# Stick-breaking attention: the running sums from rounded halves of the softplus instead of fp32 matmuls over a running total

## The reference

```
z = einsum('bqhd,bkhd->bhqk', q[:, q0:q1], k[:, :q1]) * scale
strict = k_pos[None, :] < q_pos[:, None]
log_1m = where(strict, -softplus(z), 0.0)
later = cumsum(log_1m, axis=3, reverse=True) - log_1m
w = where(strict, exp(log_sigmoid(z) + later), 0.0)
out = einsum('bhqk,bkhd->bqhd', w, v)
```

## Time and profile before

| | |
|---|---|
| time, median of 3 runs | 2959.64 us (2959.38 to 2963.29) |
| span of the profiled execution | 2957.5 us |
| the profiled execution's own time | the page gives its span alone |
| TensorE busy | 2864.2 us, 97% of the span |
| DVE, ACT, POOL busy | 36%, 43%, 39% of the span |
| DMA | 84 GB/s over the span |
| stick-breaking stage, layer 1 | from about 262 to 330 us of the span |
| stick-breaking stage, layer 2 | from about 1117 to 1184 us |

### The profile page before, as it was taken

The page is one execution under the profiler, slowest core; times in us unless marked ns, Lnnn a source line. Parts: engine busy times, 40 slices in busy tenths (PEclk is TensorE's granted clock), DMA queues, the critical chain, the costliest instruction groups (busy, mean ns, idle before and its releaser), DMA issues.

```text
span 2957.5 us, 39307 instructions
## 1 busy us (share of the span) xinstructions
PE 2864.2 (97%) x14662; PEld 2299.9 (78%) x14662; DVE 1067.7 (36%) x1405; ACT 1257.9 (43%) x1825; POOL 1141.6 (39%) x288
## 2 busy tenths in 40 slices
PE   7998999999999998999999999999998999999999
PEld 6765688888888764888888888888896678888887
DVE  6154213555222363114555034440204541244421
ACT  5356544455344356435555243332415353433322
POOL 3300355444454200554444454444531325544443
PEclk9999999999999999999999999999999999999999
DMA  6200133333324100332333233332430213323232
GB/s 169 83 12 12 43 96 114 95 90 99 106 94 116 51 12 1 85 124 86 92 95 101 98 101 95 94 99 98 119 89 20 75 34 102 117 85 99 89 108 80
DMA packets 369464, 249.78 MB, mean 84 GB/s; under 512 B 38774, under 2 KB 337478, under 8 KB 369350
## 3 DMA queue, kind: packets, MB, share of 16 engines
q1 hardware_dynamic: 366168, 246.78, 27.7%
q10 hardware_dynamic: 3182, 1.46, 0.2%
HBM read 245.74 MB, written 2.70 MB: 84 GB/s over the span
## 4 chain that ended last, share of the span: by engine, by line
PE 86%; issue 5%; ACT 4%; DVE 2%; POOL 1%; ACTq 1%; DVEq 0%; POOLq 0%
PE pair L1507 76%; PE pair L1714 1%; PE pair L1752 1%; PE pair L1735 1%; POOL wlo L499 1%; PE pair L1798 1%; PE pair L1796 1%; ACT tmp L576 1%; DVE sL L1267 1%; ACT tmp L786 0%; ACT tmp L784 0%; ACT bP L864 0%; PE pair L1784 0%; DVE hl L1014 0%; PE pair L1717 0%
## 5 line engine op out<-in xcount | busy, mean ns | idle before, releaser
L499 POOL TENSOR_TENSOR wlo<-raw,whi 128x2048 fp32r<-128x2048 f32 x235 | 1081.4, 4602 | 1790.9 <-ACT whi L540 1790.9
L1507 PE MATMUL pair<-hh,whi 128*128 128x512 f32 (+1 forms) x2256 | 881.9, 391 | 12.1 <-DVE hl L1014 8.4
L1507 PE MATMUL pair<-hl,whi 128*128 128x512 f32 (+1 forms) x2256 | 879.2, 390 | 0.0
L1507 PE MATMUL pair<-hh,wlo 128*128 128x512 f32 (+1 forms) x2256 | 879.1, 390 | 0.0
L540 ACT ACTIVATE whi<-raw 128x2048 fp32r<-128x2048 f32 x235 | 449.6, 1913 | 625.2 <-PE pair L1507 625.0
L1507 PEld LDWEIGHTS pair<-hh,whi 128*128 128x128 f32 (+1 forms) x2256 | 423.0, 188 | 107.1 <-issue 13.9
L1507 PEld LDWEIGHTS pair<-hh,wlo 128*128 128x128 f32 (+1 forms) x2256 | 423.0, 187 | 89.8
L1507 PEld LDWEIGHTS pair<-hl,whi 128*128 128x128 f32 (+1 forms) x2256 | 423.1, 188 | 88.5
L1326 DVE TENSOR_TENSOR a2lo<-tmp,a2hi 128x512 f32 x44 | 200.0, 4546 | 79.4 <-ACT a2hi L850 79.4
L1022 DVE SCALAR_TENSOR_TENSOR pair<-pair,gp_d 128x512 f32<-128x512 f32 x32 | 22.3, 698 | 407.9 <-ACT sq L548 407.6
L1507 PE MATMUL pair<-wlo,a1hi 128*128 128x512 f32 x352 | 136.9, 389 | 0.0
(11 more groups left out here) (303 smaller groups left out, 3769.4 us busy)
## 6 DMA issues: line engine op xcount, KB each, us to landing
raw<-in_w_in SPq DMA_DIRECT2D x122, 512.0 KB, 3.9
raw<-in_w_up SPq DMA_DIRECT2D x88, 512.0 KB, 4.3
raw<-in_ffn_w_gate SPq DMA_DIRECT2D x44, 512.0 KB, 3.7
raw<-in_ffn_w_up SPq DMA_DIRECT2D x44, 512.0 KB, 4.7
raw<-in_w_down SPq DMA_DIRECT2D x40, 512.0 KB, 3.8
raw<-in_ffn_w_down SPq DMA_DIRECT2D x40, 512.0 KB, 3.8
raw<-in_w_out SPq DMA_DIRECT2D x24, 512.0 KB, 4.5
raw<-in_w_proj_nsa SPq DMA_DIRECT2D x16, 256.0 KB, 4.0
```

Of the source, the lines that this page charges most:

```text
L499: pool.tensor_tensor(wlo[:, s, :], raw[:, s, :], whi[:, s, :].bitcast(f32), ALU.subtract).then_inc(lo_ready, 1)
L1507: o = pe.matmul(out, l, r, start=start and first, stop=stop and last)
```

## The change

The running total is no longer formed. The softplus stays in place in `sE`; DVE writes its rounded half (an fp32r copy) and then the remainder (a subtraction, also fp32r) into a tile that holds both halves, one tile per key block (`sLt[j]`, and a second one for the last block, `sL3b`, used in turn). TensorE multiplies, in fp32r, the minus ones with both halves of every later block, and the triangle with both halves of this block. The two constant matrices come as one fp32r tile `minus`: loaded in a DMA of its own and rounded by DVE.

Matmuls of `z_minus_sums` in a pair of heads, by the width of what is streamed:

| step | before, fp32 | after, fp32r |
|---|---|---|
| 128 | 2 of 128 | 4 of 128 |
| 256 | 2 of 128, 2 of 256 | 4 of 128, 4 of 256 |
| 384 | 2 of 256, 2 of 384 | 4 of 128, 4 of 256, 4 of 384 |
| 512 | 2 of 384, 2 of 512 | 4 of 128, 4 of 256, 4 of 384, 4 of 512 |

```diff
-            sp.dma_start(cst[:, CONST_FIRST:], consts[:, CONST_FIRST:]).then_inc(S.const_rest, 16)
+            sp.dma_start(cst[:, CONST_FIRST:], consts[:, CONST_FIRST:CONST_N]).then_inc(S.const_rest, 16)
+            sp.dma_start(minus_s[:, :, :], consts[:, CONST_N:].rearrange("p (a c) -> p a c", a=2)).then_inc(S.minus_in, 16)
...
+        def sb_L(t, j):
+
+            return sL3b if j == TT - 1 and t % 2 else sLt[j]
...
                     if n >= 2:
-                        act.wait_ge(S.L_ready, SBN * l + n - 1)
+                        act.wait_ge(S.Llo_ready, SBN * l + n - 1)
...
-            dve.memset(negones[:, :], -1.0).then_inc(S.negones_set, 1)
...
+            dve.wait_ge(S.minus_in, 16)
+            dve.tensor_copy(minus[:, :, :], minus_s[:, :, :])
...
                     dve.wait_ge(S.l_done, SBN * l + n + 1)
-                    if n >= 2:
-                        dve.wait_ge(S.arg_done, SBN * l + n - 1)
-                    L, Ls = sL[:, n % 2], sLs[:, n % 3]
-                    dve.scalar_tensor_tensor(L[:, :, 0:w], pair[n % 3][:, :, 0:w], 0.0, sE[n % 2][:, :, 0:w], ALU.max, ALU.add).then_inc(S.L_ready, 1)
-                    if j > 0:
-                        dve.drain()
-                        o = dve.tensor_copy(Ls[:, :, 0:P], L[:, :, 0:P])
-                        if j < TT - 1:
-                            o = dve.tensor_tensor(Ls[:, :, P:w], L[:, :, P:w], sLs[:, (n - 1) % 3, :, 0:w - P], ALU.add)
-                        o.then_inc(S.Ls_ready, 1)
+                    e, L = sE[n % 2][:, :, 0:w], sb_L(t, j)
+                    dve.scalar_tensor_tensor(e, pair[n % 3][:, :, 0:w], 0.0, e, ALU.max, ALU.add).then_inc(S.L_ready, 1)
+                    dve.drain()
+                    if j == TT - 1 and t >= 2:
+                        dve.wait_ge(S.arg_done, SBN * l + TT * (t - 1))
+                    elif j < TT - 1 and t >= 1:
+                        dve.wait_ge(S.arg_done, SBN * l + TT * t)
+                    dve.tensor_copy(L[:, 0], e).then_inc(S.Lhi_ready, 1)
+                    dve.drain()
+                    dve.tensor_tensor(L[:, 1], e, L[:, 0].bitcast(f32), ALU.subtract).then_inc(S.Llo_ready, 1)
...
                     pe.wait_ge(S.L_ready, SBN * l + n + 1)
-                    if j < TT - 1:
-                        pe.wait_ge(S.Ls_ready, (TT - 1) * 4 * l + (TT - 1) * t + TT - 1 - j)
+                    for k in range(TT - 1, j, -1):
+                        for part in range(2):
+                            for hf in range(2):
+                                pe.matmul(pair[n % 3][:, hf, (k - j) * P:w], minus[:, 1], sb_L(t, k)[:, part, hf], start=False, stop=True, skip_group_check=True)
+                    for part, there in enumerate((S.Lhi_ready, S.Llo_ready)):
+                        pe.wait_ge(there, SBN * l + n + 1)
                         for hf in range(2):
-                            pe.matmul(pair[n % 3][:, hf, P:w], negones[:, :], sLs[:, (n - 1) % 3, hf, 0:w - P], start=False, stop=True, skip_group_check=True)
-                    for hf in range(2):
-                        o = pe.matmul(pair[n % 3][:, hf, 0:w], C("negtri"), sL[:, n % 2, hf, 0:w], start=False, stop=True, skip_group_check=True)
+                            o = pe.matmul(pair[n % 3][:, hf, 0:w], minus[:, 0], sb_L(t, j)[:, part, hf], start=False, stop=True, skip_group_check=True)
                     o.then_inc(S.arg_done, 1)
```

More of the change, by code:

```diff
@@ L35, in _columns @@
     return cols, at
-CONST_COLS, CONST_N = _columns((("ident", P), ("invfreq", 1), ("sinsign", 1), ("unused", 30), ("negtri", P), ("causal", P), ("strictneg", P),
+CONST_COLS, CONST_N = _columns((("ident", P), ("invfreq", 1), ("sinsign", 1), ("unused", 30), ("causal", P), ("strictneg", P),
                                 ("cmpadd", TT * NCMP), ("cmpmul", TT * NCMP), ("unused_end", 8)))
@@ L63, in shape_constants @@
 def shape_constants():
-    c, c2 = np.zeros((P, CONST_N), np.float32), np.zeros((P, CONST2_N), np.float32)
+    c, c2 = np.zeros((P, CONST_N + 2 * P), np.float32), np.zeros((P, CONST2_N), np.float32)
     def put(name, a):
@@ L72, in shape_constants @@
     put("ident", np.eye(P))
-    put("negtri", np.where(r[:, None] >= r[None, :], -1.0, 0.0))
+    c[:, CONST_N:CONST_N + P] = np.where(r[:, None] >= r[None, :], -1.0, 0.0)
+    c[:, CONST_N + P:] = -1.0
     put("causal", np.where(r[None, :] <= r[:, None], 0.0, NEG))
@@ L115, in keep, with __enter__, get, __exit__ @@
             return ctx.enter_context(nc.sbuf_tensor(name, shape, dt))
+        class Region:
+            def __enter__(self):
+                self.stack = ExitStack()
+                self.stack.__enter__()
+                return self
+            def get(self, name, shape, dt=f32):
+                return self.stack.enter_context(nc.sbuf_tensor(name, shape, dt))
+            def __exit__(self, *a):
+                self.stack.__exit__(*a)
         cst = keep("cst", [P, CONST_N])
         diag = keep("diag", [P, 2, P])
-        negones = keep("negones", [P, P])
+        minus = keep("minus", [P, 2, P], f32r)
         ident_bf = keep("ident_bf", [P, P], bf16)
@@ L136, in build @@
         sq = keep("sq", [P, 2, T])
+        with Region() as r:
+            sL3b = r.get("sL3b", [P, 2, 2, P], f32r)
         acc = keep("acc", [P, T])
@@ L146, in build @@
         ident = C("ident")
[L148 to L160, removed]
         hh = keep("hh", [P, KT, T], f32r)
@@ L189, in build @@
                 xg_s = q.get("xg_s", [P, XG, D])
+                minus_s = q.get("minus_s", [P, 2, P])
             with Region() as q:
@@ L218, in build @@
                 with Region() as n:
-                    sL = n.get("sL", [P, 2, 2, T])
-                    sLs = n.get("sLs", [P, 3, 2, 3 * P])
-                    n.get("gap_sb", [P, 256])
+                    sLt = [n.get(f"sL{j}", [P, 2, 2, T - j * P], f32r) for j in range(TT)]
                     sW = n.get("sW", [P, 3, 2, T])
@@ L304, in build @@
         for name in """const_in const_rest const2_in table_in pos_in gp_in gq_in zeros_set toep_zero toep_filled
-            tables_t tables_copied ang_ready sin_done tables_ready negones_set
+            tables_t tables_copied ang_ready sin_done tables_ready minus_in
             tok_done sq0_done sq1_done half_set root1_done root2_done x_ready xg_ready diag_set turned hh_ready h_ready
@@ L309, in build @@
             nsa_scores nsa_max nsa_exp nsa_scaled nsa_transposed nsa_copied nsa_pv nsa_ohi nsa_ofree
-            sqk_act sqk_dve z_done l_done L_ready Ls_ready arg_done w_ready spv_done so_hi so_lo
+            sqk_act sqk_dve z_done l_done L_ready Lhi_ready Llo_ready arg_done w_ready spv_done so_hi so_lo
             gates_set y_set y2_hi y_ready
@@ L1614, in add_zeros @@
                                  ident_bf[:, :].rearrange("p (o c) -> p o c", o=1).broadcast_to([P, TT, P]), start=start, stop=not start)
-            pe.wait_ge(S.negones_set, 1)
             pe.wait_ge(S.const_in, 16)
```

## The result

The changed kernel took 2964.4 us (median of 20 runs, 2960.74 to 2972.09) against 2961.21 (20 runs, 2956.3 to 2965.8): ratio 1.0018, 95% interval 1.0012 to 1.0023. So it got slower by 3.6 to 6.8 us. The 0.18% lies inside the 0.2% that I had called no change, though the interval reaches beyond it; it lies inside the range, but on the other side of zero from the forecast of -5.3 us. The profiled executions are further apart, 2965.5 and 2957.5 us. One execution of e7 took 5683.01 us and is in no ratio; all the others were fast.

A forecast was written before the change was run, and what follows sets the result against it. The page's chain bounds the kernel, with the stage's 512 and 256 steps on it: 8 x (-0.72 - 0.14) = -6.9, plus 1.6 for the clock, gives -5.3 us, a median of 2954.3. Range: 2950.5 to 2968.

The forecast's parts named there:

- What bounds the stage: Stick-breaking stage: the 512 and 256 steps are on the chain, and a microsecond gained there is gained at the end.
- The price of a narrow fp32r matmul: TensorE's sums: a 128-column fp32r matmul, which no row showed, was taken at 0.12 us.
- The rival of slow narrow ones: Sums on TensorE: 128-column fp32r matmuls gain nothing, 0.356 us each, +8.6 us in all: 2968.2; chance 0.17.
- the copy rival: DVE's rounding copy runs at the two-source rate, so the sum is only -1.4 us: 2958.3; chance 0.08.
- The rounding copy: On DVE: assumed as fast as a plain copy, 0.42 us for 512 elements and 0.68 for 1024.
- The 512 step: Its sums on the chain, from the end of L: 2.60 us in place of 3.32, -0.72 each, eight of them.
- The 256 step: Its sums on the chain, with the remainder waited for: 1.48 us in place of 1.62, -0.14 each, eight of them.
- The steps in the gaps and the start: The 128 and 384 steps stay hidden in waits; the start costs nothing, half a microsecond as bound either way.
- The clock: TensorE's granted clock in the stages: one fall more than before, +1.6 us; bounds -1.6 and +4.7.
- the clock falls in every pair of heads: Rival, TensorE's clock in the stages: eight falls, seven more, +11.1 - 6.9 = +4.2 us: 2963.8; chance 0.08.

The follow-up runs named there:

- e7: The changed kernel with z of step n + 2 issued ahead of the values of step n - 1: ratio 0.9984 to the kernel before.
- e1: The changed kernel with five zero-adding matmuls on TensorE before the wait for L of each 512 step: 2958.39 us against 2958.12 for the kernel before.
- e5: The changed kernel with five zero-adding matmuls before each 512 step and z of step 2 issued three times: ratio 0.9994 to the kernel before.
- e9: The changed kernel with z ahead of the values, the five fillers and z of step 2 three times: 2944.82 us against 2959.03 for the kernel before.
- e10: The changed kernel with two zero-adding matmuls on TensorE ahead of each 512 step: ratio 0.9995 to the kernel before.
- e4: The changed kernel without the remainders, only the rounded half made and multiplied: ratio 0.9976 to the kernel before.

## Why the prediction was wrong, point by point

- **What bounds the stage**: right. The same two steps stayed on the chain, and what the stage lost, the run lost: 62.49 to 66.43 us in layer 1 from the second sums to L1514 (267.82 to 334.25), 60.90 to 66.46 in layer 2, +9.5; the rest of the profiled span gave back 1.5.
- **The price of a narrow fp32r matmul**, which I had called the first thing to go wrong: right. Four of them and the wait's restart took 292.09 - 291.59 = 0.50 us in e1, 0.125 each for the 0.12 I took (0.16 us from the first start to the second, 0.11 from there on); the following eight, of 256 and 384 columns, 1.22 for 1.17:

```profile
291.59 0.66 PE L1805 MATMUL pair<-sL3b,minus 128*128 128x128 f32 x4 [0.26 <-DVE tmp L1272]
292.09 1.39 PE L1805 MATMUL pair<-sL,minus 128*128 128x256 f32 x8
293.31 1.11 PE L1809 MATMUL pair<-sL,minus 128*128 128x512 f32 x4
```

  The rival of slow narrow ones is out. Its 0.356 was also a misreading: the 0.71 us of the fp32 row run to the end of the last record, and from start to start the four took 301.32 - 300.77 = 0.55, so 0.275 a matmul. Its sum, like that of the copy rival, leaves out the fall that the forecast had. The Trainium skill ("TensorE: Matmul & The Clock Gate", LDWEIGHTS) gives 107 ns for the weight load, from which my estimate of 0.107 came; the trace's 0.11 in the stream agrees.
- **The rounding copy**: right, 0.70, 0.43 and 0.29 us for 1024, 512 and 256 elements, at the rate of the earlier trace rows. That rival is out too:

```profile
277.91 0.70 DVE L1278 CAST sL<-tmp 128x1024 fp32r<-128x1024 f32 x1
278.69 1.23 DVE L1280 TENSOR_TENSOR sL<-tmp,sL 128x1024 fp32r<-128x1024 f32 x1
280.08 0.42 DVE L1272 SCALAR_TENSOR_TENSOR sq<-pair,sq 128x256 f32<-128x256 f32 x1 [0.16 <-issue]
280.60 0.29 DVE L1278 CAST sL3b<-sq 128x256 fp32r<-128x256 f32 x1
```

- **The 512 step**, -0.72: it won 3.28 - (1.89 + 0.95) = 0.44. The term was mis-sized by 0.28. The twelve minus ones took 279.60 - 277.87 = 1.73 us of the timeline for my 1.65, the four triangle matmuls 280.64 - 279.60 = 1.04 for 0.90 (the last of them 0.33 up to the first of the values, where one of a stream takes 0.23), and the chain counts 0.07 more to the end of the last record.
- **The 256 step**, -0.14: it lost 0.24 (285.10 to 286.96, against 1.62). A gap of 0.09 stood between DVE's instructions where I had 0.05, twice; and the last two matmuls, behind a wait of their own, took 0.50 on the chain for my 0.24 (0.22 from the first start to the second, 0.12 to the next in the stream, and the chain counts to the end of the record). A wait in front of two matmuls costs more than the rate of a stream tells.
- The two make -0.20 us a pair for the -0.86 of the sum: -1.6 us for -6.9. e5 agrees, 72.5 to 71.7 a layer.
- **The steps in the gaps and the start**: right, nothing of them came to the chain; the copy of `minus` took 0.28 of the 0.43 that DVE had.
- **The clock is the step that failed.** I put "one fall more than before: +1.6", with three more as the bound. There were seven more in the profile, and two of the eight were long. At the 512 steps a fall cost 17.14 - 15.59 = 1.55 us, as priced; six of those make 9.3 us. What I named as a rival with 0.08, "the clock falls in every pair of heads", with +4.2 us, is what happened, but for the first pair. I had dismissed it because full pairs ran at 1.00 "with a wait of the same length"; that wait was 0.94 us in the middle pairs of before and became 1.32. The 0.38 is what the 384 step's shorter sums leave empty: from its neighbour's mask to its values TensorE took 290.81 - 288.13 = 2.68 us before and 290.85 - 288.55 = 2.30 after. So the wait had to grow with the change itself, and the prediction gave that growth no number. The mechanism of the page that I had weighed against layer 2 held: the Trainium skill ("TensorE: Matmul & The Clock Gate", A second HAM failure mode) tells of short idle times between groups of matmuls and a clock that goes to and fro, and the trace agrees, with eight falls.
- The sum with what the profile showed: -1.6, +9.3, and for the longer falls at the starts +0.4 and +2.0 (from the second to the fourth sums 277.87 - 267.82 = 10.05 and 1138.03 - 1127.96 = 10.07 us, against 9.64 and 8.06) make +10.1 for the stages' +9.5. Of the 15.4 us between my -5.3 and this +10.1, the clock has 10.1 (11.7 for 1.6) and the two steps' mis-sized terms 5.3. Without the clock's share the change would have been a gain of 1.6 us, as in e5.

## What to carry to other kernels

Where TensorE waits on other engines in a loop and runs at its full clock, making its work there shorter lengthens its idle time, and the clock can fall just where the chain needs it, as it did here in six of eight 512 steps; price a change there with the clock at either level, and look at the granted clock of stretches cut at the waits. Then fill the idle time, best with work that leaves the chain (e7, e9), or with matmuls of zeros (e1), which also tells whether a slowdown is the clock's. A split into halves pays only if the remainder is made beside other work; each wait in front of a few short matmuls costs a restart.

## What the runs showed of the hardware that was not expected

- The same twelve matmuls, 1.89 and 3.34 us, in one chain: at a granted clock of 1.00 (2.4 GHz) and of 0.50 (1.2 GHz).
- Matmuls of zeros ahead of a wait keep the clock: five, or two (0.45 us of work), took away all falls at those steps (e1, e10).
- Less busy does not mean more falls: 33.8 busy of 44.4 us at a clock of 1.00 in e4, 13.5 us a round, against a fall in every round but the first in the profile of the changed kernel, with more work in it.
- An fp32r matmul of 128 columns takes 0.11 us of a stream (0.125 with the restart after a wait), and one of 256 takes 0.12: with half the columns the time hardly shrinks.
